# A forgetting attention that runs one unit deeper beside the projections, and gates taken as one plus tanh straight from PSUM

## The reference

```
z  = RMSNorm(x) @ w_in      # q | k | v | forget | pooling input u | memory query | 3 branch gates of 1024
branch A: forgetting attention, 8 heads x 64, logit[t,s] += sum_{s<j<=t} log f_j, s <= t
branch B: pooling means, w_pool, s_pool
branch C: attention of 4 heads x 128 over 256 memory tokens
h = x + W_out( sum_b sigmoid(gate_b(xn)) * W_b(branch_b) )
x = h + W_down( relu(RMSNorm(h) @ W_up)^2 ), then a last RMSNorm
```

## Time and profile before

| | |
|---|---|
| time, median of 3 runs | 2186.33 us (2182.19 to 2186.51) |
| the profiled execution's own time | 2186.78 us |
| its span, first to last instruction | 2185.0 us |
| TensorE matmul busy | 2078.0 us, 95% of the span, 12111 instructions |
| weight load busy | 1997.4 us, 91% |
| DVE busy | 993.8 us, 45% |
| ACT busy | 690.1 us, 32% |
| DMA | 164.75 MB, mean 75 GB/s |
| mean granted TensorE clock | 0.98 |

### The profile page before, as it was taken

The page is one execution under the profiler, slowest core; times in us unless marked ns, Lnnn a source line. Parts: engine busy times, 40 slices in busy tenths (PEclk is TensorE's granted clock), DMA queues, the critical chain, the costliest instruction groups (busy, mean ns, idle before and its releaser), DMA issues.

```text
span 2185.0 us, 29163 instructions
## 1 busy us (share of the span) xinstructions
PE 2078.0 (95%) x12111; PEld 1997.4 (91%) x12111; DVE 993.8 (45%) x1876; ACT 690.1 (32%) x1214; POOL 6.9 (0%) x37
## 2 busy tenths in 40 slices
PE   6898999999998998899989999999999999999997
PEld 6897888988887887889989999999999999999997
DVE  6454524334244554556433345544444444443434
ACT  7324515334254544554322233211111111111112
POOL 0000000000000000000000000000000000000000
PEclk9999999999999998999999999999999999999998
DMA  6611121111214543234332331111111111102112
GB/s 186 156 34 61 34 92 36 65 37 50 81 31 166 169 137 133 88 98 154 111 96 76 108 83 50 39 30 53 34 49 39 41 47 34 55 28 58 30 49 96
DMA packets 211784, 164.75 MB, mean 75 GB/s; under 512 B 14399, under 2 KB 190527, under 8 KB 211142
## 3 DMA queue, kind: packets, MB, share of 16 engines
q1 hardware_dynamic: 211653, 162.90, 24.5%
HBM read 133.36 MB, written 29.51 MB: 75 GB/s over the span
## 4 chain that ended last, share of the span: by engine, by line
PE 65%; ACT 3%; DVE 3%; issue 2%; DMA 1%; SPq 0%; DVEq 0%; ACTq 0%
PE ps L1039 56%; PE ps L894 2%; PE ps L907 2%; PE ps L866 1%; PE ps L919 1%; DMA merged<-prod 0%; PE ps L910 0%; PE ps L816 0%; PE ps L976 0%; ACT w_hi L408 0%; PE ps L832 0%; PE ps L1120 0%; PE ps L1000 0%; DVE prod L1814 0%; DMA branch_raw<-o_mem 0%
## 5 line engine op out<-in xcount | busy, mean ns | idle before, releaser
L1039 PE MATMUL ps<-act_hi,w_hi 128*128 128x384 f32 x1824 | 624.9, 343 | 1.6 <-DVE w_lo L415 1.6
L1039 PE MATMUL ps<-act_hi,w_lo 128*128 128x384 f32 x1824 | 614.4, 337 | 0.0
L1039 PE MATMUL ps<-act_lo,w_hi 128*128 128x384 f32 x1824 | 614.2, 337 | 0.0
L1039 PEld LDWEIGHTS ps<-act_hi,w_hi 128*128 128x128 f32 x1824 | 346.2, 190 | 3.9 <-DVE w_lo L415 1.8
L1039 PEld LDWEIGHTS ps<-act_lo,w_hi 128*128 128x128 f32 x1824 | 346.2, 190 | 0.3
L1039 PEld LDWEIGHTS ps<-act_hi,w_lo 128*128 128x128 f32 x1824 | 345.5, 189 | 0.0
L408 ACT ACTIVATE w_hi<-w_raw 128x512 fp32r<-128x512 f32 (+1 forms) x181 | 152.8, 844 | 383.9 <-PE ps L1039 375.7
L1039 PE MATMUL ps<-ff_hi,w_hi 128*128 128x384 f32 x768 | 259.5, 338 | 0.0
L1039 PE MATMUL ps<-ff_lo,w_hi 128*128 128x384 f32 x768 | 259.4, 338 | 0.0
L1039 PE MATMUL ps<-ff_hi,w_lo 128*128 128x384 f32 x768 | 259.4, 338 | 0.0
L415 DVE TENSOR_TENSOR w_lo<-w_raw,w_hi 128x512 fp32r<-128x512 f32 (+1 forms) x181 | 174.6, 964 | 143.1 <-ACT w_hi L408 143.1
(11 more groups left out here) (318 smaller groups left out, 2845.9 us busy)
## 6 DMA issues: line engine op xcount, KB each, us to landing
w_raw<-in_w_in_dram SPq DMA_DIRECT2D x45, 512.0 KB, 4.6
w_raw<-in_w_up_dram SPq DMA_DIRECT2D x32, 512.0 KB, 4.2
w_raw<-in_w_down_dram SPq DMA_DIRECT2D x64, 256.0 KB, 2.8
merged<-prod SPq DMA_DIRECT2D x48, 192.0 KB, 1.9
prev<-merged SPq DMA_DIRECT2D x48, 192.0 KB, 3.7
foxs_kraw<-in_cache_fox_k_dram SPq DMA_DIRECT2D x8, 1024.0 KB, 5.4
foxs_vraw<-in_cache_fox_v_dram SPq DMA_DIRECT2D x8, 1024.0 KB, 5.7
out_dram<-fin_y SPq DMA_DIRECT2D x9, 512.0 KB, 2.6
```

The lines of the kernel that those rows point to most:

```text
L1039: last = nc.tensor.matmul(bank(b)[:, 0:width], W[k][a][:, t, :], moving[z][:, t, j * width:(j + 1) * width], start=(t == 0 and n == 0), st ...
```

## The change

Four things are changed together.

1. In the prompt's attention turn moves from place s+1 to s+2 of its unit and values from odd to even places, one later; there are 19 places, and the 19th stands at the next pass's first q half (or the first half of `qm`). There are three buffers `fp` for two. On ACT a unit's normalise stands at the head of the next place, and on odd places the exponential behind the high part; on DVE the reciprocal moves to the head of the next place.
2. TensorE no longer waits at place 0 for the last block of `vturn`, but at place 4, ahead of the first values.
3. The gates: sigmoid(x) is (1 + tanh(x/2))/2. ACT takes tanh of each block from PSUM, for all three branches; DVE computes (tanh + 1) times the product in one instruction; the halves are made good where the sum over the branches is split (`scale=0.5`). The copy and the separate sigmoid are gone.
4. SP starts the load of the samples' first keys at place 17, ahead of the last pass's store of `fo`, which moves to place 18; the four loads of `refill(0)` move by one half; `tok`, `kst`, `QS` and `KS` move in memory to make room, and so the setting of `ones` comes later.

```diff
+        put(("q", p + 1, 0, 0) if p + 1 < BT else ("qm", 0, 0, 0), "fox", p, 18)
...
-        fp = [tensor(f"fox_p{k}", [P, SEQ], R_AT + 4096 * k) for k in range(2)]
+        fp = [tensor(f"fox_p{k}", [P, SEQ], R_AT + (4096 * k if k < 2 else 73728)) for k in range(3)]
...
             def fox(p, s):
-                if s == 17:
+                if s == 17 and p == BT - 1:
+                    sp.wait_ge(at_s["t_over"], UNITS)
+                    load_keys(samples[0], 0)
+                if s == 18:
                     sp.wait_ge(at_s["o_done"], 8 * (p + 1))
                     sp.dma_start(o_fox[:, p, :], fo[:]).then_inc(at_s["o_stored"], 16)
                     if p == BT - 1:
-                        sp.wait_ge(at_s["t_over"], UNITS)
-                        load_keys(samples[0], 0)
                         sp.wait_ge(at_s["pv_over"], PAIRS)
...
-                if s == 0:
-                    emptied(pe, at["vturn", p, 0].b + 2)
                 if s < 16:
                     scores(s)
-                if s >= 3 and s % 2:
-                    values(s - 2)
-                if 1 <= s <= 16:
-                    turn(s - 1)
+                if s >= 4 and s % 2 == 0:
+                    if s == 4:
+                        emptied(pe, at["vturn", p, 0].b + 2)
+                    values(s - 3)
+                if 2 <= s <= 17:
+                    turn(s - 2)
...
-                if s < 16:
-                    exponent(u, fp[s % 2][:, 0:n], fp[s % 2][:, 0:n], -1.0)
                 if 1 <= s <= 16:
-                    turned_parts(u - 1, fpt, (s - 1) % QT + 1)
-                if s < 16:
-                    normalise(u, fp[s % 2][:, 0:n])
+                    normalise(u - 1, p_of(u - 1))
+                if s < 16 and s % 2 == 0:
+                    exponent(u, p_of(u), p_of(u), -1.0)
+                if 2 <= s <= 17:
+                    turned_parts(u - 2, fpt, (u - 2) % QT + 1)
+                if s < 16 and s % 2:
+                    exponent(u, p_of(u), p_of(u), -1.0)
...
-                        nc.scalar.activation(g[:], g[:], ACT.Sigmoid).then_inc(mg["sig"], 1)
...
-                    nc.scalar.activation(gate1[:, cols(j)], src, ACT.Sigmoid).then_inc(free, 1)
+                        emptied(act, at["br", s.i, s.j - 1].b + j)
+                    elif s.i == 2:
+                        emptied(act, at["br", 1, KT - 1].b + j)
+                    elif s.i == 1 and j == 0:
+                        for n in range(2):
+                            act.wait_ge(tok_stored[n], tok_by[n])
+                    nc.scalar.activation((gate1 if s.i else gate0)[:, cols(j)], src, ACT.Tanh,
+                                         scale=0.5).then_inc(free, 1)
...
+                if 1 <= s <= 16:
+                    reciprocal(u - 1)
                 if s < 16:
...
-                    reciprocal(u)
-                if 1 <= s <= 16:
-                    turned_parts(u - 1, fpt, (s - 1) % QT + 1)
-                if s >= 3 and s % 2:
-                    h, i = divmod(s - 2, QT)
-                    j = (u - 2) // 2
+                if 2 <= s <= 17:
+                    turned_parts(u - 2, fpt, (u - 2) % QT + 1)
+                if s >= 4 and s % 2 == 0:
+                    h, i = divmod(s - 3, QT)
+                    j = (u - 3) // 2
...
-                elif s.kind == "gate" and s.i < 2:
-                    finished(dve, b)
...
-                    nc.vector.tensor_copy((gate1 if s.i else gate0)[:, cols(j)], src).then_inc(free, 1)
...
-                    nc.vector.tensor_tensor(dst[:], src, gate[:, cols(j)], ALU.mult).then_inc(free, 1)
+                    nc.vector.scalar_tensor_tensor(out=dst[:], in0=gate[:, cols(j)], scalar=1.0, in1=src, op0=ALU.add,
+                                                   op1=ALU.mult).then_inc(free, 1)
```

More of the change, by code:

```diff
@@ L275, in encoder_program @@
         vf = tensor("fox_vf", [P, T], R2_AT + 24576)
-        tok = [tensor(f"tok{k}", [P, 3, P], R3_AT + 1536 * k) for k in range(2)]
-        kst = [tensor(f"kst{k}", [P, NMEM], R3_AT + 3072 + 1024 * k) for k in range(2)]
-        QS = parts("qs", [P, BT, P], R3_AT + 5120)
-        KS = parts("ks", [P, BT, P], R3_AT + 9216)
+        tok = [tensor(f"tok{k}", [P, 3, P], R3_AT + 1920 + 1536 * k) for k in range(2)]
+        kst = [tensor(f"kst{k}", [P, NMEM], R3_AT + 4992 + 1024 * k) for k in range(2)]
+        QS = parts("qs", [P, BT, P], R3_AT + 7040)
+        KS = parts("ks", [P, BT, P], R3_AT + 11136)
         sf = dict(kraw=tensor("foxs_kraw", [P, ST, 512], R_AT), vraw=tensor("foxs_vraw", [P, ST, 512], R_AT + 8192),
@@ L354, in encoder_program @@
                    "v_hi", "v_lo", "pv_over", "om", "ot_over", "o_hi", "o_done", "block", "block_step", "max")
-        mg = group("merge", "sig", "added", "hi", "lo")
+        mg = group("merge", "added", "hi", "lo")
         prod_stored = [sem(f"prod_stored{k}") for k in range(2)]
@@ L626, in _ @@
                         load_weights(sp, s.c + 2)
-                    if s.kind == "qm" and s.i == 0 and x == 0:
+                    if s.kind == "qm" and s.i == 0 and x == 1:
                         refill(0)
@@ L715, in _ @@
                 nc.gpsimd.memset(cnt_col[:, t:t + 1], 1.0 / (t + 1))
-            nc.gpsimd.memset(ones[:], 1.0)
             nc.gpsimd.memset(f_m3[:], 1.0)
@@ L747, in _ @@
             pool.wait_ge(me["q_lo"], MH)
+            nc.gpsimd.memset(ones[:], 1.0)
             head_blocks(samples[1])
@@ L1342, in leave @@
                         act.wait_ge(mg["added"], 3 * KT + i + 1)
-                        nc.scalar.activation(M[0][:, s.j, cols(j)], prod1[i % 2][:], ACT.Copy).then_inc(mg["hi"], 1)
-                    return
-                if s.kind == "gate" and s.i < 2:
-                    if j == 2:
-                        emptied(act, b)
-                        g = gate1 if s.i else gate0
-                        nc.scalar.activation(g[:], g[:], ACT.Sigmoid).then_inc(mg["sig"], 1)
+                        nc.scalar.activation(M[0][:, s.j, cols(j)], prod1[i % 2][:], ACT.Copy, scale=0.5).then_inc(mg["hi"], 1)
                     return
@@ L1408, in leave @@
                     if s.j:
-                        act.wait_ge(mg["added"], 3 * KT + 3 * (s.j - 1) + j + 1)
-                    else:
-                        act.wait_ge(mg["added"], 3 * KT)
-                    nc.scalar.activation(gate1[:, cols(j)], src, ACT.Sigmoid).then_inc(free, 1)
+                        emptied(act, at["br", s.i, s.j - 1].b + j)
[6 more added lines that the diff above has]
+                                         scale=0.5).then_inc(free, 1)
                 elif s.kind == "forget":
@@ L1796, in leave @@
                                                    op1=ALU.subtract).then_inc(free, 1)
-                elif s.kind == "gate" and s.i < 2:
-                    finished(dve, b)
-                    if s.i == 1 and s.j == 0 and j == 0:
-                        for n in range(2):
-                            dve.wait_ge(tok_stored[n], tok_by[n])
-                    nc.vector.tensor_copy((gate1 if s.i else gate0)[:, cols(j)], src).then_inc(free, 1)
                 elif s.kind == "br":
                     i = 3 * s.j + j
+                    emptied(dve, at["gate", s.i, s.j].b + j)
                     if s.i < 2:
-                        dve.wait_ge(mg["sig"], KT * s.i + s.j + 1)
                         n = 12 * s.i + i // 2
```

19 lines of the change are left out of this document (11 added, 8 removed).

## The result

| | before | changed | ratio, 95% interval |
|---|---|---|---|
| first chip, median of 4 and 4 runs | 2185.97 us | 2147.78 us (2143.62 to 2152.8) | 0.9823 [0.9802, 0.9843] |
| second chip, median of 9 and 4 runs | 2187.7 us | 2145.35 us (2141.19 to 2146.5) | 0.9804 [0.9789, 0.9820] |

What follows compares the result with a forecast made beforehand. TensorE, 95% busy, bounds the kernel; time comes only from its waits and slow clock. 7.2 + 6.7 + 10.2 + 6.7 + 7 + 3.5 = 41.3 off 2186.8 gives 2145.5; forecast 2145 us, range 2133 to 2161.

Steps and rivals of the forecast that it cites:

- Table loads and turns: TensorE's waits at turns and values in the passes: 12.8 us falls to 5.6, gain 7.2, bounds 0 and 12.8.
- Start of a pass: TensorE's wait for `vturn`'s third block at passes 1 to 3: 10.9 us less 3 x 1.4, gain 6.7, bounds 3 and 10.9.
- The clock: TensorE's clock stays at 1.00 at the starts of passes 1 to 3: gain 10.2 us, bounds 0 and 10.2.
- The first rival: The clock still falls at pass starts, after idle time within `vturn`'s transposes; falls cost 7 to 10: 2154 us, chance 0.14.
- The samples' start: Waits for the samples' first keys and the clock's fall at 687.2 go: gain 6.7 us, bounds 2 and 7.2.
- more is gained: Rival: the low clock stretch from 834 on goes too and the memory's waits shrink by 10: 2137 us, chance 0.11.
- The memory's stretch: About 5.5 of 15.3 us of waits and the clock's fall at 857.8 go: gain 7, bounds 2 and 12.
- the 3.5: Each removed TensorE wait gives 0.15 us more than its row; some 25 waits, 3.5 us.
- The cost of tanh: Each tanh of 384 columns on ACT takes 0.49 us, covered by the next place's scores and 12 matmuls (2.1 us).
- the rival's 2200: Rival at the gates: tanh needs its own table loads, 48 pairs of 2.6 us, about 2200 us, chance 0.01.

Runs made afterwards that it cites:

- Experiment 1: The kernel before with only the new gates (tanh of each block from PSUM, one plus tanh times the product), attention in its old order: 2165.4 us, ratio 0.9894.
- Experiment 6: The changed kernel with block 15's reciprocal and normalising issued at the end of place 15 instead of at place 16: 2139.39 us, ratio 0.9780.
- experiment 3: The changed kernel with TensorE's wait for the last block of `vturn` put back at place 0 of each pass: 2155.74 us, ratio 0.9852.
- 7: The changed kernel with 8 unused matmuls in the wait ahead of the last three value turns at the starts of passes 1 to 3: 2140.23 us, ratio 0.9786.
- experiment 8: The changed kernel with 13 unused transposes in the wait ahead of the last three value turns at the starts of passes 1 to 3: 2142.3 us, ratio 0.9797.
- Experiment 4: The changed kernel with the load of the samples' first keys put back behind the store of the last pass's output, at place 18: 2151.63 us, ratio 0.9831.
- 2: The changed kernel with the old gates (copy by DVE, one sigmoid of 1152 columns with its table loads): 2170.48 us, ratio 0.9917.

## Why the prediction was right, and where it was wrong

The time was met to 3 us, and the mechanism is the one predicted: fewer table loads ahead of the exponentials, and work put ahead of the late evacuation. One step failed, and others that were sized too small made up for it; that the sum came out so near is in part luck.

- **Table loads and turns**: predicted to go from 12.8 us to 5.6; measured 4.5 (3.4 and 1.1). The chain for turn 15 holds to a tenth: counted as in the prediction, the scores' end T is at 641.64; TensorE was to be stopped until T + 8.8, and turn 15 starts at 650.47, T + 8.8. Its wait was to be 1.0, and is 0.86 and the 0.15 that the view leaves out. Experiment 1 shows that the gates alone take the turns down; the deeper order adds nothing there, and the loads were not behind the values' waits by themselves. Experiment 6 shows that what is left hangs on the place of the reciprocal and the normalising, as the working had it.
- **Start of a pass**: predicted 4.2 us left of 10.9; measured 1.1. The order of events was right. The wait of the gate block was sized at 0.6 and is 0.28 to 0.4; that of scores 1, sized at 0.8, is not there as long as the clock is at 0.50, and is 0.36 to 0.55 in the traces where it stays up.
- **The clock**: the step that failed. "With two waits of 0.6 and 0.8, and work between them, I expect the clock to stay: gain 10.2." The stretches at the starts hold 16.7 us of work after 20.4 before, and one of 3.4 us is new at 195: of 10.2 nothing came in the first trace, about 4 in the second. The working compared single idle times and took the longest as what decides. It also misread the trace before. "A single wait of 1.5 was never followed by a fall", but the stretch from 834.0 stands behind one of 1.45, and that from 181.9 behind waits of 1.31 and 1.16:

```profile
832.35 1.16 PE L907 MATMUL ps<-foxs_v_hi,foxs_pt_hi 128*128 128x512 f32 x4 [1.45 <-DVE foxs_vn_lo L1727]
```

The runs show instead that the fall hangs on the 1.3 us among the turns, though it does not come every time (13 of 15 starts): with the 3.65 put back (experiment 3) the clock falls at all three starts as without it, with the 1.3 filled (7, 8) it does not fall. The first rival named just that idle time, at 0.14; it should have had more. The rule of the Trainium skill (TensorE: Matmul & The Clock Gate, PE-mode transpose) led to the same outcome, but by a reason that experiment 8 does not bear out.
- **The samples' start**: predicted 6.7, with 0.5 of waits left of 5.7; 1.8 are left (1.4 for the second keys, 0.3 for the queries' low part). Experiment 4 takes back 2 to 6 us by the times. The stage gained 13.3 in one trace and 9.1 in the other. What is beyond the term is the stretch from 834 on: its 12.8 us of work cost 6.4, and in the changed kernel it was absent once and 10.2 us long once. The prediction had this under "more is gained", as a lasting effect; it is one of the single execution.
- **The memory's stretch**: predicted 7 and its part of the 3.5; measured 9.3. Its waits at L987 and L978 are 9.8 us together for 15.3, which is the 5.5 predicted; besides the fall at 857.8 the one at 926.1 went as well, which no term had. Experiments 1 and 2 show that the stage hangs on the gates. Another 2.5 to 3.3 came behind it, at the memory's samples, where the wait for `branch_lo` is 6.1 for 8.2 (6.2 with the gates alone, 8.4 with the order alone); no term stood for that.
- **The cost of tanh**: 0.49 us each, as taken from the sigmoid; no wait for the gates appears in the view, so the cover named (scores and 12 matmuls) held.
- **Slips that moved nothing**: the passes have 72 places and not 64, and 48 pairs of 2.6 us would be 125 us and not the 55 of the rival's 2200.

In sum the passes gave 16.8 and 18.4 us in the two traces, where 7.2, 6.7 and 10.2 stood for them; the stages behind them gave more than their terms. In the first trace the waits in the passes fell by 18.1 us and the clock gave nearly nothing, which is 1.3 more than the stage shows; that difference was not traced. In the second the first wait of pass 0, for the forget bias, grew from 1.8 us to 3.2. The range of 28 us was as wide as the case needed: both the missing clock and the stretch from 834 on lay in it.

## What to carry to other kernels

An activation function that needs no table load beside its neighbours can pay even on an engine that is 32% busy, if another engine waits behind the loads: here 31 loads of 1.28 us gone, 40 us of ScalarE's time, took 23 us off the whole. When an evacuation is late, put independent matmuls ahead of the wait for it; then look for the short instruction (here a reciprocal of 0.16 us) that stands behind a long one on the engine that feeds the chain. Do not book a clock that "will stay" from the length of the longest idle time alone: look at all idle time ahead of the fall, at every fall that the trace has and the shortest wait ahead of one, and at whether the same kernel shows the fall in each execution. And do not book the whole price of the half clock: what TensorE does faster it may wait out behind the engine that feeds it.

## What was not expected of the hardware

- The clock at the starts of passes 1 to 3 fell in 13 of 15 cases (five traces of kernels in the changed order without filling: three starts each; experiment 3 is not among them and falls at its three as well) and in none of 18 (six traces with 1.3 us filled). A filled idle time costs nothing, but only there: from the first value turns to the last three it takes 2.15 us unfilled and 2.16 with 8 matmuls, but with 84 matmuls where TensorE has no wait the program is 9 to 11 us longer.
- 13 transposes of 128x128 held the clock at 1.00 as 8 matmuls of 128x384 did.
- The stretch of half clock ahead of the memory is between 0 and 13.6 us long in executions of almost the same instructions. In the two traces of the changed kernel the samples' stage is 165.6 us without it and 169.8 with 10.2 us of it. Runs of one kernel spread by 3 to 9 us; that such stretches make a good part of this is likely, but most of these runs have no trace.
- Kept up at three starts, the clock was worth less than the prediction's 10.2 us: beside it on the same chip the changed kernel had three stretches of 3.4 us, whose 9.55 us of work cost 4.8, and the passes with matmuls are 2.7 us shorter (462.1 for 464.8). Waits at scores 1, three with 1.3 us in all and 0.15 more each, take most of the difference.
